# Head turns moved to the output bank, and unread mask matmuls at the norm borders and in the forget attention's tail

## The reference

```python
h = rms_norm(x, g_pre)
p = h @ w_in                       # q, k, v, gate of three attentions, and the forget logits
ya = merge(diff_attention(...)) * silu(ga)            # "diff", 4 heads of 2 x 64
yb = merge(stick_breaking_attention(...)) * silu(gs)  # "sb", 8 heads of 64
yc = merge(forgetting_attention(...)) * silu(gf)      # "fox", 8 heads of 64
y = concatenate([ya, yb, yc]) @ w_out
return x + rms_norm(y, g_post)
```

## Time and profile before

| | before |
|---|---|
| median of three runs | 2033.78 us |
| the profiled execution's own time | 2034.04 us |
| its span, first to last instruction | 2032.2 us |
| TensorE busy | 1939.6 us (95%) |
| VectorE, ScalarE, GpSimd busy | 773.9, 886.7, 661.7 us |
| mean granted TensorE clock | 0.967 |
| TensorE's share of the chain that ended last | 85% |

### The profile page before, as it was taken

How to read it: one execution, slowest core, us unless ns; L and a number is a source line. 1 busy time by engine, 2 the same in 40 slices (tenths; PEclk the granted TensorE clock), 3 DMA queues, 4 the chain that set the end, 5 groups by cost and what they waited for, 6 DMA issues and landing times.

```text
span 2032.2 us, 25677 instructions
## 1 busy us (share of the span) xinstructions
PE 1939.6 (95%) x9552; PEld 1599.5 (79%) x9552; DVE 773.9 (38%) x1393; ACT 886.7 (44%) x1741; POOL 661.7 (33%) x278
## 2 busy tenths in 40 slices
PE   8998999998899999899889999999999989999998
PEld 6887887877778778787777788888788878888886
DVE  3435554444443565544445681110251431111102
ACT  4556454344455556434453742333353343323222
POOL 2422332320233222232023354344203434444442
PEclk9999999996899999999789999999999989999999
DMA  4221211211322122121042232222202413223232
GB/s 150 83 73 53 73 63 52 73 63 63 114 77 74 58 63 69 57 73 63 21 166 78 79 103 94 89 90 91 73 1 63 143 67 101 94 96 101 94 96 91
DMA packets 44572, 163.80 MB, mean 81 GB/s; under 512 B 6192, under 2 KB 6448, under 8 KB 43824
## 3 DMA queue, kind: packets, MB, share of 16 engines
q1 hardware_dynamic: 42640, 148.65, 22.0%
q10 hardware_dynamic: 1824, 13.63, 1.8%
HBM read 155.97 MB, written 6.29 MB: 80 GB/s over the span
## 4 chain that ended last, share of the span: by engine, by line
PE 85%; DVE 7%; ACT 4%; issue 3%; DMA 0%; POOL 0%; DVEq 0%; ACTq 0%; POOLq 0%; SPq 0%
PE bank L577 12%; PE bank L579 12%; PE bank L578 12%; PE bank L580 11%; PE bank L582 10%; PE bank L581 10%; PE bank L690 3%; PE bank L714 2%; PE bank L708 2%; PE bank L668 2%; PE bank L669 1%; PE bank L710 1%; ACT q_dup L903 1%; PE bank L666 1%; PE bank L630 1%
## 5 line engine op out<-in xcount | busy, mean ns | idle before, releaser
L560 POOL TENSOR_TENSOR w_hl<-w_raw,w_hl 128x1024 fp32r<-128x1024 f32 x274 | 661.5, 2419 | 1346.3 <-ACT w_hl L791 1345.8
L791 ACT ACTIVATE w_hl<-w_raw 128x1024 fp32r<-128x1024 f32 x274 | 287.3, 1057 | 331.2 <-DMA w_raw<-wstream 330.6
L577 PE MATMUL bank<-act_hl,w_hl 128*128 128x512 f32 x1056 | 427.2, 405 | 2.8 <-DVE act_hl L1134 2.1
L579 PE MATMUL bank<-act_hl,w_hl 128*128 128x512 f32 x1056 | 413.7, 392 | 0.0
L578 PE MATMUL bank<-act_hl,w_hl 128*128 128x512 f32 x1056 | 413.2, 391 | 0.0
L580 PE MATMUL bank<-w_hl,act_hl 128*128 128x512 f32 x672 | 267.6, 398 | 5.2 <-POOL w_hl L560 2.4
L581 PE MATMUL bank<-w_hl,act_hl 128*128 128x512 f32 x672 | 264.0, 393 | 0.0
L582 PE MATMUL bank<-w_hl,act_hl 128*128 128x512 f32 x672 | 264.0, 393 | 0.0
L577 PEld LDWEIGHTS bank<-act_hl,w_hl 128*128 128x128 f32 x1056 | 199.9, 189 | 45.3 <-DVE act_hl L1134 2.6
L579 PEld LDWEIGHTS bank<-act_hl,w_hl 128*128 128x128 f32 x1056 | 199.3, 189 | 43.3
L578 PEld LDWEIGHTS bank<-act_hl,w_hl 128*128 128x128 f32 x1056 | 200.0, 189 | 40.1 <-issue 1.9
(11 more groups left out here) (216 smaller groups left out, 2906.5 us busy)
## 6 DMA issues: line engine op xcount, KB each, us to landing
w_raw<-wstream SPq DMA_DIRECT2D x274, 512.0 KB, 3.4
x_spill<-x_res ACTq DMA_DIRECT2D x2, 2048.0 KB, 7.9
x_res<-x_spill ACTq DMA_DIRECT2D x2, 2048.0 KB, 8.0
x_res<-x SPq DMA_DIRECT2D x4, 512.0 KB, 4.9
g_post<-post_gains ACTq DMA_DIRECT2D x4, 512.0 KB, 3.8
x_res<-x ACTq DMA_DIRECT2D x1, 2048.0 KB, 7.7
out<-x_res SPq DMA_DIRECT2D x4, 512.0 KB, 2.6
probs<-w_gates ACTq DMA_DIRECT2D x1, 1024.0 KB, 9.7
```

The lines of the kernel that those rows point to most:

```text
L560: nc.gpsimd.tensor_tensor(w_hl[:, slot, 1].rearrange("p c n -> p (c n)"), w_raw[:, slot, :], w_hl[:, slot, 0].rearrange("p c n -> p (c n)" ...
L577: pe.matmul(out_ap, wh, ah, start=start, stop=False)
L579: return pe.matmul(out_ap, wl, ah, start=False, stop=stop)
L791: nc.scalar.activation(w_hl[:, b % RING, 0].rearrange("p c n -> p (c n)"), w_raw[:, b % RING, :], ACT.Copy).then_inc(s_high_done, 1)
```

## The change

The head turns of diff, sb and fox go through `BO` (bank 7) instead of `BT` (bank 6); those of dil stay. A helper `keep_busy(done, n)` waits until the bank user `done` is drained and issues `n` matmuls of 512 columns on bf16 mask data into bank 0, which nobody reads. At borders 1 to 3, in `norm_turn` part 0, there are 10 before the first tile, 5 before each of the other three and 4 after the last. In fox, at steps 13 to 17, there are 4 in part 0 (after the scores, where there are any) and 4 in part 1.

```diff
--- before.py
+++ after.py
@@ -229,7 +229,7 @@
                     mark("rms", (l, kind, value))
             if n in HEADS_AT[kind] and part == 1:
                 p = HEADS_AT[kind].index(n)
-                take(("Y", l, kind, p), BT)
+                take(("Y", l, kind, p), BT if kind == "dil" else BO)
                 mark("y_high", (l, kind, p))
                 mark("y_low", (l, kind, p))
     return steps, groups, blocks, use, marks
@@ -618,12 +618,23 @@
                 if tiles[-1] == 3:
                     mm.then_inc(s_block_used, 1)
 
+            def keep_busy(done, n):
+
+                pe.wait_ge(*drained(done))
+                for _ in range(n):
+                    pe.matmul(bank[0][:, :], mask_b[:, len(MASKS), :], mask_b[:, 0:4, :].rearrange("p a n -> p (a n)"),
+                              start=True, stop=True)
+
             def norm_turn(i, part):
 
+                if i > 0 and part == 0:
+                    keep_busy(("dense", LAST[i - 1], 0), 10)
                 for c in NORM_CHUNKS[part]:
                     if earlier(("norm", i, c))[1] > 0:
                         pe.wait_ge(*earlier(("norm", i, c)))
                 for t in range(TT):
+                    if part == 0 and i > 0 and t > 0:
+                        keep_busy(("dense", LAST[i - 1], 0), 5)
                     if part == 0:
                         pe.wait_ge(s_h_rows, i * TT + t + 1)
                     for c in NORM_CHUNKS[part]:
@@ -631,6 +642,8 @@
                                        diag[:, t, :], start=True, stop=True)
                         if t == TT - 1:
                             tr.then_inc(filled(("norm", i, c)), 1)
+                if i > 0 and part == 0:
+                    keep_busy(("dense", LAST[i - 1], 0), 4)
 
             def forget(l):
                 if earlier(("ff", l))[1] > 0:
@@ -762,11 +775,15 @@
                             ready(pe, l, kind, 1)
                         if n < 16:
                             scores(l, kind, n)
+                        if kind == "fox" and 13 <= n < 18:
+                            keep_busy(("dense", group("g", l=l, kind=kind)["index"], 0), 4)
                         if 0 <= n - 1 < 16:
                             turn(l, kind, n - 1, 0)
                         if 0 <= n - 2 < 16:
                             values(l, kind, n - 2)
                     else:
+                        if kind == "fox" and 13 <= n < 18:
+                            keep_busy(("dense", group("g", l=l, kind=kind)["index"], 0), 4)
                         if 0 <= n - 1 < 16:
                             for a in value_maps(kind)[1:]:
                                 turn(l, kind, n - 1, a)
```

## The result

The changed kernel takes 2016.62 us (median of four runs, 2014.13 to 2019.41) against 2032.88 us for the kernel before (median of four, the three of the table and 2031.97); the ratio is 0.9920 with a 95% interval of 0.9905 to 0.9935. That is 16.3 us less, 13 to 19 by the interval. Forecast were 2019.6 us and a range of 2009 to 2028. The profiled execution took 2014.13 us, 2.5 under its median, and that of the kernel before 2034.04 us, 1.2 over its median. So the two traces lie 19.9 us apart, 3.6 more than the medians, and what is read off the pair is generous by that much.

A forecast was written before the change was run, and what follows sets the result against it. Taken as bound by TensorE, with half-clock time at three borders and two fox tails and head-turn waits to win. Borders -5.4, sb -6.5, diff +8.6, tails -11.1 make -14.4 us on 2034.04: 2019.6 us, range 2009 to 2028.

The forecast's parts named there:

- The fox tail: Scores of step 13 to output product, per layer: full clock with masks cuts 26.31 us to 21.6, -4.7.
- inside: Fox tails: what moved head turns save of the wait for L1322 was counted within the tails' -11.1 us, not separately.
- the one figure of 11.1: Both fox tails with step 12 and the output product's start: -7.6 us in one, -3.5 in the other, -11.1 together.
- Price of a mask: One 512-column mask matmul on TensorE: 0.23 us at full clock, 0.43 at half, the upper bounds taken.
- The rival with 0.13: Fox tails: a mask costs 0.13 us, less than a dense matmul; the 80 give 8 us, 2012 us; chance 0.03.
- The borders: Three borders between layer parts: masks keep the clock, 0.3 + 1.5 = 1.8 us saved at each, -5.4 us.
- Sb: Sb head turns no longer wait for L1322; idle of 0.93, 1.62 and 0.69 us goes, 3.24 per layer, -6.5 us.
- Diff: Diff head turns wait for their later-drained new bank: 3.4 us per layer, plus 1.8 for half clock in one layer, +8.6.
- The masks as pure cost: Fox tails and borders: half clock stays or returns, masks only add time; +43 us, 2077 us; chance 0.10.
- Tails set by ScalarE and VectorE: Fox tails keep 26.3 us, not bound by TensorE; only the product's 1.1 is gained; 2028.5 us; chance 0.11.
- the two cases on the clock in step 12: Fox, before the masks: clock held from step 12, -7.6 us, or fallen before step 13, -3.5; one tail of each taken.
- The +2.4 us for a step 13 at half clock: Fox tail: if the clock falls first, step 13's scores, four masks and a turn run at half clock, +2.4 us.

## Why the prediction was right, point by point

**The fox tail** was right in its parts. Predicted were 11.3 us of TensorE work and 9.1 us of masks, 20.4 in all; measured 20.36. Predicted idle 1.2, measured 21.55 - 20.36 = 1.19; length 21.6 and 21.55. TensorE sets this length only in part: with half the masks, 3.3 us of work less gave 0.7 (above). What the sum hid under "inside" was a term of its own: at full clock, fox's moved turns are worth 2.2 us per tail (23.77 to 21.57). Both effects were meant to be in the one figure of 11.1, and the run with the fox turns and the tail masks alone gave 11.0 us, beside the 11.1 of the sum.

The 9.1 for 40 masks is a slip, 40 x 0.23 being 9.2, and at the measured price they are 8.7, so some 11.7 of the 20.36 are other work.

**Price of a mask.** Four in a row last 1.03 us with 0.38 for the last, so they start (1.03 - 0.38) / 3 = 0.217 us apart. I had taken 0.23, from bounds of 0.18 and 0.23. The rival with 0.13, the figure of the Trainium skill ("TensorE: Matmul & The Clock Gate", section "Back-to-back issue gap"), is out.

**The borders** were sized at 1.8 each: 0.3 ahead of the product and 1.5 in its first eight matmuls. At border 1 the first part is 10.80 - 10.59 = 0.2 and the second 3.40 - 1.9 = 1.5, as forecast. The fifth mask ahead of the last tile is late, as forecast: that turn begins at 521.19 with no idle, its diagonal (start 520.65, 0.28 long) being ready at 520.93. The whole border, from the first norm turn to the first of part 1, before and after:

```profile
521.91:539.74 17.83, 14.77 (x56) 12.49 (x57) 8.70 (x12) 9.11 (x21) 2.37 (x1) 0.62 0.43 168
...
513.32:529.45 16.13, 13.92 (x74) 10.08 (x76) 8.69 (x12) 9.11 (x21) 2.38 (x1) 1.00 0.46 184
```

That is 1.7 us; borders 2 and 3 went from 17.89 to 16.11 and from 18.40 to 16.17, and the three give 5.7 in these traces, where 5.4 was forecast. In all six kernels with these masks at the borders, 18 borders took 16.11 to 16.17 us. Of the 21 borders without masks in seven kernels 17 took 17.8 to 18.6 us, but four took 16.3 to 16.4: there the half clock did not reach the product, and there is almost nothing to win. That fits the 3.7 us (1.6 to 5.9) that the borders alone measured; how often a border is spared in the runs that were not profiled is not known.

**Sb** was sized at 6.5. Alone it measured 7.7, with tails and a border in it that are not its own. In the stretches of sb it gave 4.0 us per layer alone, and 3.9 and 4.0 in the changed kernel, 8 in all. The mechanism is as forecast; each of the three turns saved 0.2 to 0.3 us more than its idle time, which the forecast put at nothing.

**Diff** was sized at 6.8 for the waits and 1.8 for the clock, 8.6 in all. In the changed kernel the two diffs cost 3.9 and 3.6 us, 7.5 in all. The 1.8 was right in kind: behind the stall of layer 0 the clock halved, since the matmuls start 0.43 us apart from 164.90 on:

```profile
164.66 0.44 PE L577 MATMUL bank<-act_hl,w_hl 128*128 128x512 f32 x1
164.90 0.63 PE L578 MATMUL bank<-act_hl,w_hl 128*128 128x512 f32 x1
165.33 0.63 PE L579 MATMUL bank<-act_hl,w_hl 128*128 128x512 f32 x1
```

In the whole change the diff turns cost some 11 us, alone 1.8. The trace of diff alone shows where: its stalls of 3.7 and 3.3 us are there, and its tails, which have no masks, are shorter by nearly as much than those of the kernel before. With the masks on, the tails ran at full clock from step 13 whether diff's turns were moved or not, and gave nothing back. The tails of the run with sb's turns alone are as short, so it takes no moved diff turn to make them so. Whether the shift of the work made them so, or chance, no run separates.

**Head turns alone** were forecast at no difference (-6.5, +8.6 and a little for fox) and gave -0.4. In its trace sb's 7.8 us and diff's 6.8 nearly cancel. But one kind at a time the turns gave -7.7 (sb), +1.8 (diff) and -2.2 (fox), -8.1 in sum, and that is further from -0.4 than the four intervals allow together (some 5.4). So the kinds do not add when there are no masks: each run alone holds what its tails and borders did with the clock, as shown for sb and diff.

**The rivals.** The masks as pure cost, 2077 us, is out by 60 us. Tails set by ScalarE and VectorE, which would have kept 26.3 us, is out: they took 23.77 with the masks alone and 21.55 with both. Of the two cases on the clock in step 12 neither came whole: in the profiled execution the clock was lower in step 12 of layer 0 (0.62 in this stretch) and full in both tails from step 13 on:

```profile
461.00:464.40 3.40, 3.13 (x12) 1.95 (x12) 2.04 (x6) 0.84 (x5) 0.00 (x0) 0.62 0.02 5
```

The step of the forecast that failed in form is the one that tied low clock in step 12 to low clock in step 13. It fell and came back before step 13 in layer 0; in layer 1 step 12 was at full clock as well (4.02 us at 1.00, before 6.29 at 0.55). In the run with all masks and the turns unmoved it did last into step 13, and the tail took 26.08 us. As a mean the two cases served less well than the sum looks: the sum's 11.1 us is 5.5 per tail, of which the stretch itself gave 4.76 (26.31 to 21.55). With step 12 and the start of the product the traces show 6.5 us in layer 0 and 8.0 in layer 1. The +2.4 us for a step 13 at half clock was not paid in either layer.

**What was luck in the number.** The terms of the sum, beside the same stretches in the two traces:

| | forecast, us | the two traces, us |
|---|---|---|
| borders | -5.4 | -5.7 |
| sb | -6.5 | -7.9 |
| diff | +8.6 | +7.5 |
| tails with step 12 | -11.1 | -14.5 |
| all else | 0 | +0.7 |
| sum | -14.4 | -19.9 |

The mechanism of each term is right and each has the right sign, but all four came out better than forecast in these two executions, which lie further apart than the medians (16.3 us). "All else" is not nothing: the kernel started 1.2 us late, and a stretch of layer 0's sb, between the head turns of steps 13 and 16, took 9.85 us at 1.00 in the changed kernel and 13.06 at 0.74 before. No mask and no moved turn stands in it. In the twelve other kernels it took 13.1 us in six and 11.5 in the other six, whatever their edits. Such stretches of half clock come and go without a part of the change being in them, and the kernel before by itself shows mean clocks from 0.966 to 0.974 over its runs. That the measured 16.3 us and the forecast 14.4 lie only 1.9 apart is in part luck.

## What to carry to other kernels

Unread matmuls pay where TensorE waits for a chain of other engines and the granted clock falls behind the wait; here 512 columns kept the clock at full through a border (1.00 where 64 columns had 0.79) and through the tails, and the waits around them decide what is left of the gain. They do not undo a fall that comes ahead of them. Before a result is moved to another bank, ask for each kind of work what the new bank's previous drain waits for: here the same edit saved 4.0 us per layer in sb and lost 3.7 in diff, since diff's drain stands behind ScalarE's three steps of a norm and VectorE's work on a later unit. Leaving diff alone gives 2005 us, 1.3% under the kernel before, and two masks a group gave the same time as four (ratios 0.9868 and 0.9867).

## What the runs showed of the hardware that I had not expected

Without masks, tails of the same instructions differ widely, in one execution as well as between kernels: with fox's turns unmoved eight tails of four kernels took 24.20 to 27.03 us, at mean clocks of 0.72 to 0.56, and with the turns moved four tails of two kernels took 22.23 to 25.82, at 0.82 to 0.60. With four masks a group from step 13 and the moved turns the six tails of three kernels took 21.55 to 21.57. The masks made this stretch repeat itself, and not only shorter, as long as the half clock did not reach into step 13. Single profiles of kernels that let the clock fall are thus weak evidence for differences of a few us: I took one for a cause and was wrong (the masks in the tails alone).

Mask matmuls of 64 columns still gained 4.7 us (2.4 to 6.7 by the interval), though the clock fell around them. Their trace has it at the borders: the clock was at half while TensorE waited anyway, and back at full for the product. Where a half clock falls decides what it costs. Whether the short masks made it fall there is open.
